# Prompt attention in 64 steps of two query tiles each, with q and k stored as halves by their projection

## The reference

```python
def stick_breaking(q, k, v, sb_bias, q_pos, k_pos):
    z = jnp.einsum('bqhd,bkhd->bhqk', q.astype(jnp.float32), k.astype(jnp.float32)) * (HEAD_DIM_SB ** -0.5)
    z = z + sb_bias.astype(jnp.float32)[None, :, None, None]
    mask = k_pos[None, :] < q_pos[:, None]
    log_1mb = jnp.where(mask, jax.nn.log_sigmoid(-z), 0.0)
    suffix = lax.cumsum(log_1mb, axis=3, reverse=True) - log_1mb
    a = jnp.where(mask, jnp.exp(jax.nn.log_sigmoid(z) + suffix), 0.0)
    o = jnp.einsum('bhqk,bkhd->bqhd', a, v.astype(jnp.float32))
    return o.astype(v.dtype)
```

## Time and profile before

| | us |
|---|---|
| runs, median (lowest to highest) | 3154.99 (3153.28 to 3155.18) |
| the profiled execution | 3153.76 |
| its span, first to last instruction | 3152.2 |
| attention stage, first sigmoid to the next stage's first transfer | 549.27 to 1198.18 |

### The profile page before, as it was taken

How to read it: one execution, slowest core, us unless ns; L and a number is a source line. 1 busy time by engine, 2 the same in 40 slices (tenths; PEclk the granted TensorE clock), 3 DMA queues, 4 the chain that set the end, 5 groups by cost and what they waited for, 6 DMA issues and landing times.

```text
span 3152.2 us, 51506 instructions
## 1 busy us (share of the span) xinstructions
PE 3035.5 (96%) x18364; PEld 2805.3 (89%) x18364; DVE 2062.2 (65%) x2820; ACT 1645.0 (52%) x2375; POOL 149.1 (5%) x277
## 2 busy tenths in 40 slices
PE   8999999888888889999999999999999999999998
PEld 6888887776677669999999999999999999999998
DVE  4222422888987897775677756777477774778845
ACT  5444311997888885543445534455344543444433
POOL 0000000112311220000000000000000000000000
PEclk9999999999999999999999999999999999999999
DMA  5224334554755555443364334543445434444432
GB/s 185 93 93 137 108 114 120 139 135 133 202 129 134 137 169 156 118 120 112 110 183 120 114 114 130 164 119 111 116 142 154 115 113 117 143 127 120 115 112 78
DMA packets 584224, 405.90 MB, mean 129 GB/s; under 512 B 38489, under 2 KB 547842, under 8 KB 584034
## 3 DMA queue, kind: packets, MB, share of 16 engines
q1 hardware_dynamic: 543012, 301.45, 33.8%
q0 software_dynamic: 20544, 67.19, 7.4%
q10 hardware_dynamic: 20512, 35.17, 3.2%
HBM read 358.87 MB, written 44.87 MB: 128 GB/s over the span
## 4 chain that ended last, share of the span: by engine, by line
PE 62%; DVE 0%; issue 0%; DVEq 0%; ACT 0%; ACTq 0%
PE pf_acc L60 20%; PE pf_acc L58 20%; PE pf_acc L59 20%; PE pf_ps_t L1720 1%; PE pf_ps_sum L1659 0%; PE pf_ps_sum L1668 0%; PE pf_ps_sum L1673 0%; PE pf_ps_t L1730 0%; PE pf_ps_t L1791 0%; DVE late_c L2066 0%; DVE late_ssum L1998 0%; DVEq L1596 0%; DVE late_u L1988 0%; DVE pf_h L2192 0%; ACT late_sq L1819 0%
## 5 line engine op out<-in xcount | busy, mean ns | idle before, releaser
L1812 ACT ACTIVATE late_w_hi<-ahead_raw 128x1024 fp32r<-128x1024 f32 x439 | 463.8, 1057 | 536.7 <-PE pf_acc L60 533.9
L60 PE MATMUL pf_acc<-pf_x_hi,late_w_lo 128*128 128x416 f32 x2080 | 734.1, 353 | 0.0
L58 PE MATMUL pf_acc<-pf_x_hi,late_w_hi 128*128 128x416 f32 x2080 | 733.1, 352 | 0.0
L59 PE MATMUL pf_acc<-pf_x_lo,late_w_hi 128*128 128x416 f32 x2080 | 726.0, 349 | 0.0
L1982 DVE TENSOR_TENSOR late_w_lo<-ahead_raw,late_w_hi 128x1024 fp32r<-128x1024 f32 x439 | 536.1, 1221 | 269.8 <-ACT late_w_hi L1812 269.0
L58 PE MATMUL pf_acc<-late_f_hi,late_w_hi 128*128 128x416 f32 x1280 | 453.4, 354 | 3.2 <-DVEq L2205 3.2
L60 PE MATMUL pf_acc<-late_f_hi,late_w_lo 128*128 128x416 f32 x1280 | 451.9, 353 | 0.0
L59 PE MATMUL pf_acc<-late_f_lo,late_w_hi 128*128 128x416 f32 x1280 | 447.6, 350 | 0.0
L59 PEld LDWEIGHTS pf_acc<-pf_x_lo,late_w_hi 128*128 128x128 f32 x2080 | 390.8, 188 | 7.9 <-issue 1.6
L58 PEld LDWEIGHTS pf_acc<-pf_x_hi,late_w_hi 128*128 128x128 f32 x2080 | 390.5, 188 | 3.7 <-issue 1.6
L60 PEld LDWEIGHTS pf_acc<-pf_x_hi,late_w_lo 128*128 128x128 f32 x2080 | 390.0, 187 | 2.3
(11 more groups left out here) (248 smaller groups left out, 3971.9 us busy)
## 6 DMA issues: line engine op xcount, KB each, us to landing
ahead_raw<-in_w_up_dram SPq DMA_DIRECT2D x220, 512.0 KB, 4.0
ahead_raw<-in_w_down_dram SPq DMA_DIRECT2D x80, 512.0 KB, 4.0
high_pages<-in_cache_k_dram POOLq DMA_DIRECT2D x128, 256.0 KB, 3.5
ahead_raw<-in_w_out_dram SPq DMA_DIRECT2D x40, 512.0 KB, 5.3
ahead_raw<-in_w_ple_gate_dram SPq DMA_DIRECT2D x40, 512.0 KB, 4.0
high_pages<-in_cache_v_dram POOLq DMA_DIRECT2D x64, 256.0 KB, 3.4
at_kT<-in_cache_v_dram POOLq DMA_DIRECT2D x64, 256.0 KB, 4.1
ahead_raw<-in_w_down_dram SPq DMA_DIRECT2D x40, 384.0 KB, 3.5
```

The lines of the kernel that those rows point to most:

```text
L58: nc.tensor.matmul(out, stat_hi, mov_hi, start=first, stop=False)
L59: nc.tensor.matmul(out, stat_hi, mov_lo, start=False, stop=False)
L60: return nc.tensor.matmul(out, stat_lo, mov_hi, start=False, stop=last)
L1812: nc.scalar.activation(w_hi[k % 4][:, :], raw[k % 4][:, :], ACT.Copy).then_inc(hi_split, 1)
```

## The change

Query tiles m and 15-m make one step: together they have 17 key tiles for every m, so there are 64 steps of 2176 columns. The columns stand in the order long tile, short tile, and a step has three granules of 768, 768 and 640 columns (`EDGES`). VectorE runs two running products in a step, one for each tile, and one weighting. A step has five groups of transposes (4, 4, 4, 4 and 1 tiles), and these now alternate with the granules. `project_qk` splits q and k after its transposes and stores both halves (QH, QL, KH, KL); `load_operands` fetches them with six transfers for each head (the first head's first 1536 columns already in `project_qk`), and `operands` and `keys_high` are gone. `units_of` spreads the units evenly over the steps 3 to 61. Some small buffers and the work that prepares the next stage are moved. The core of the diff:

```diff
+def load_operands(eng, D, tiles, h, cols, loaded):
+    q2, k_hi, k_lo = (f32(t[:, cols]) for t in tiles)
+    rows = slice(64 * h, 64 * h + 64)
+    for part in range(2):
+        half = slice(64 * part, 64 * part + 64)
+        eng.dma_start(q2[half, :], D[("QH", "QL")[part]][rows, cols]).then_inc(loaded, 16)
+        eng.dma_start(k_hi[half, :], D["KH"][rows, cols]).then_inc(loaded, 16)
+        eng.dma_start(k_lo[half, :], D["KL"][rows, cols]).then_inc(loaded, 16)
...
-                sp.dma_start(dst[:, :, bass.ds(at, P)], src[s][:, :, :]).then_inc(stored[s], 16)
+                sp.dma_start(to_hi[:, :, bass.ds(at, P)], hi[s][:, :, :]).then_inc(stored[s], 16)
+                sp.dma_start(to_lo[:, :, bass.ds(at, P)], lo[s][:, :, :]).then_inc(stored[s], 16)
...
+                    dve.wait_ge(stored[s], 32 * stores)
+                banked = src[:, :].rearrange("p (k t) -> p k t", k=4)
+                nc.vector.tensor_copy(hi[s][:, :, :].bitcast(F32R), banked).then_inc(high, 1)
+                dve.wait_ge(high, n)
+                nc.vector.tensor_tensor(lo[s][:, :, :].bitcast(F32R), banked, hi[s][:, :, :], ALU.subtract).then_inc(ready, 1)
...
-            q2, q_raw, half = front["q2"], front["q_raw"], slice(0, 1024)
-            dve.wait_ge(raw_loaded, 64)
-            nc.vector.tensor_copy(q2[:, half], q_raw[:, :]).then_inc(q_high, 1)
...
-            dve.wait_ge(q_high, 1)
-            nc.vector.tensor_tensor(q2[64:P, half], q_raw[64:P, :], f32(q2[64:P, half]), ALU.subtract)
-            dve.wait_ge(k_high, 1)
-            nc.vector.tensor_tensor(front["k_lo"][:, half], front["k_raw"][:, :], f32(front["k_hi"][:, half]), ALU.subtract)
...
     HEADS, NQ, LAG = 8, 16, 3
-    STEPS = HEADS * NQ
+    PER = NQ // 2
+    STEPS = HEADS * PER
+    TILES, GRANULES, RUNS = NQ + 1, 3, 5
+    WIDTH = P * TILES
+    EDGES = (0, 768, 1536, WIDTH)
...
+    def short_tile(s):
+        return s % PER if s // PER == HEADS - 1 else PER - 1 - s % PER
+    def long_tile(s):
+        return NQ - 1 - short_tile(s)
...
-    total_keys = sum(keys_of(s) + 300 for s in range(3, STEPS - 2))
     units_of = [[] for _ in range(STEPS + LAG + 2)]
-    t, run, placed = 3, keys_of(3) + 300, 0
+    t, placed, first_unit, last_unit = 3, 0, 3, STEPS - 3
     for g in range(GROUPS):
         for u in range(UNITS):
             if apart(u) and units_of[t]:
-                for _ in range(2 if u in (U_TURN, U_MIX) else 1):
-                    t += 1
-                    run += keys_of(t) + 300
-            while t < STEPS - 3 and run * GROUPS * UNITS < placed * total_keys:
+                t += 2 if u in (U_TURN, U_MIX) else 1
+            while t < last_unit and (t + 1 - first_unit) * GROUPS * UNITS < placed * (last_unit - first_unit):
                 t += 1
-                run += keys_of(t) + 300
             units_of[t].append((g, u))
             placed += 1
...
-    def first_turns(t):
+    def turns(t):
         s = t - LAG
-        return min(groups[s], max(1, 3 - len(turned_fills(t)))) if has(s) else 0
+        if not has(s):
+            return [range(0)] * (GRANULES + 1)
+        first = max(1, 3 - len(turned_fills(t)))
+        ends = [first, first + 1, first + 2, RUNS]
+        return [range(a, b) for a, b in zip([0] + ends, ends)]
     order = []
...
+                def load(h):
+                    if h >= 2:
+                        sp.wait_ge(z_ready, granule(PER * (h - 1), 0))
+                    load_operands(sp, D, [t[h % 2] for t in (q2, k_hi, k_lo)], h, slice(0, 2048), qk_loaded[h % 2])
...
                 def logits(s, g):
-                    i, h = s % NQ, s // NQ
...
+                    border = P * (long_tile(s) + 1)
+                    for c in range(EDGES[g], EDGES[g + 1], BANK):
+                        end = min(c + BANK, EDGES[g + 1])
+                        parts = [(c, min(end, border), long_tile(s), c)] if c < border else []
+                        if border < end:
+                            parts.append((max(c, border), end, short_tile(s), max(c, border) - border))
+                        parts.sort(key=lambda part: part[1] - part[0])
+                        for a, b, tile, k0 in parts:
+                            w, z0 = max(b - a, 2 * P), a - EDGES[g]
+                            turned = b - a == P and b - c == BANK
+                            last = scores(z, z0 - P if turned else z0, w, q2[h % 2][:, tile * P:(tile + 1) * P], h, k0, turned, b in (border, WIDTH))
+                            if b in (border, WIDTH):
+                                last = nc.tensor.matmul(z[:, b - P - EDGES[g]:b - EDGES[g]], ident_b[:, :], far_b[:, :], start=False, stop=True)
                     last.then_inc(z_ready, 1)
...
+                            tiles = long_tile(s + e) + 1
+                            kt, end, at = (n, tiles - 1, P) if n < tiles else (n - tiles, NQ - tiles, 0)
+                            last = nc.tensor.matmul(ps_o[64 * e:64 * e + 64, at:at + P], v[h % 2][:, kt, :], aT[(s + e) % 3][:, n, :],
+                                                    start=kt == 0, stop=kt == end, tile_position=(0, 64 * e))
...
-                        for r in range(first_turns(t)):
+                    for g in range(GRANULES + 1):
+                        for r in turns(t)[g]:
                             turn(s, r)
-                    if has(t):
-                        for g in range(granules[t]):
+                        if has(t) and g < GRANULES:
                             logits(t, g)
-                    if has(s):
-                        for r in range(first_turns(t), groups[s]):
-                            turn(s, r)
+                    if has(s - 2) and s % 2 == 0:
...
                 def sigmoid(t, g):
-                    n = keys_of(t)
-                    at = granule(t, g)
-                    w = min(n - 1024 * g, 1024)
+                    at, h = granule(t, g), t // PER
+                    c0, w = EDGES[g], EDGES[g + 1] - EDGES[g]
                     act.wait_ge(z_ready, at + 1)
-                    nc.scalar.activation(beta[t % 3][:, 1024 * g:1024 * g + w], ps_z[at % 2][:, 0:w], ACT.Sigmoid, bias=bias[t // NQ % 2][:, :])
-                    c0, skip = (0, 1) if g == 0 else (1023, 0)
+                    nc.scalar.activation(beta[t % 3][:, c0:c0 + w], ps_z[at % 2][:, 0:w], ACT.Sigmoid, bias=bias[:, h:h + 1])
+                    c0, skip = (0, 1) if g == 0 else (c0 - 1, 0)
                     nc.scalar.activation(rest[t % 4][:, c0:c0 + w - skip], ps_z[at % 2][:, skip:w], ACT.Sigmoid, scale=-1.0,
-                                         bias=minus_bias[t // NQ % 2][:, :]).then_inc(b_done, 1)
...
-                    if has(s):
-                        for r in range(first_turns(t)):
+                    for g in range(GRANULES + 1):
+                        for r in turns(t)[g]:
                             take(s, r)
-                    if quad_end(s - 2):
-                        quad_out((s - 2) // 4)
-                    if has(t):
-                        sigmoid(t, 0)
-                    if has(s):
-                        for r in range(first_turns(t), groups[s]):
-                            take(s, r)
-                    if has(t) and granules[t] == 2:
-                        sigmoid(t, 1)
-                    if t % NQ == PART_AT[0] and t // NQ + 1 < HEADS:
-                        keys_high(2 * (t // NQ + 1))
-                    if t % NQ == PART_AT[1] and t < STEPS:
-                        keys_high(2 * (t // NQ) + 1)
-                    if t == STEPS:
+                        if g == 0 and pair_end(s - 2):
+                            pair_out((s - 2) // 2)
...
-                        act.wait_ge(a_done, STEPS)
                         act.wait_ge(join["raw_loaded"][0], 16)
...
-                    if t == STEPS + 2:
+                    if t == STEPS + LAG + 1:
...
-                def operands(n, part):
-                    slot = n // 2 % 2
-                    src = slice(0, HALF)
-                    cols = slice(n % 2 * HALF, n % 2 * HALF + HALF)
-                    if part == 0:
-                        dve.wait_ge(loaded, 64 * n + 64)
-                        nc.vector.tensor_copy(q2[slot][:, cols], q_raw[:, src]).then_inc(q_high, 1)
-                    if part == 1:
-                        dve.wait_ge(q_high, n + 1)
-                        nc.vector.tensor_tensor(q2[slot][64:P, cols], q_raw[64:P, src], f32(q2[slot][64:P, cols]), ALU.subtract)
-                        if n % 2 == 0 and n:
-                            biases_of(n // 2)
-                    if part == 2:
-                        dve.wait_ge(k_high, n + 1)
-                        nc.vector.tensor_tensor(k_lo[slot][:, cols], k_raw[:, src], f32(k_hi[slot][:, cols]), ALU.subtract).then_inc(half_ready, 1)
...
+                    end = P * (long_tile(s) + 1)
+                    dve.wait_ge(b_done, granule(s, [end <= edge for edge in EDGES].index(True) - 1) + 3)
```

(4 more changed lines are left out.)

242 lines of the change are left out of this document (101 added, 141 removed).

## The result

The changed kernel takes 3203.12 us (median of 4 runs, 3195.55 to 3206.12) against 3155.09 of the kernel before on the same chip: the ratio is 1.0149, with an interval of 1.0130 to 1.0167. It is 48 us slower. The forecast of 3160, and with it the whole range up to 3185, was too low.

What follows compares the result with a forecast made beforehand. No engine is full; TensorE and ScalarE take turns as the bound. Stage +1.1, start +1.4 and tail -2.6 make 0; 5 us for the clock gives 3158.8, and the median's 1.2 gives 3160, range 3112 to 3185 (own 3148 to 3172).

Steps and rivals of the forecast that it cites:

- the walk: Attention stage stepped through by instruction prices: 15.4 us for two equal steps without units, 628.2 us for the stage.
- VectorE's dropped work: Attention stage: 15 casts and 30 subtractions fewer on VectorE, costed at nothing; busy time lower by some 45 us.
- The two places: Steps 26 and 55: eight sums in a row wait for pages of values, some 16 us lost in each.
- the clock: TensorE's clock falling in the attention stage, mostly idle at the page waits; 5 us added to the forecast.
- Then pairs with two sums at 18.3: Step pairs behind the eight sums in a row, with two sums in each step: 18.3 us per pair.
- the sentence on the next head's load: SyncE's load of the next head, 3 MB instead of 2 MB, stands ahead of this head's stores and lands in time.
- the start: End of `project_qk`: last subtraction and a second transfer delay the end of that stage by some 1.4 us.
- the tail: From the last sigmoid to the next stage: 19.2 us against 21.8 before, so -2.6.
- rival 2: Sums in steps 26 and 55: pages are not waited for, or other engines' lists fill the time; 3130, chance 0.15.
- rival 3: Attention stage: ten more clock falls of 3.4 us, +17, giving 3176; decides below mean clock 0.94; chance 0.25.
- Its other place: Odd steps where TensorE waits for the third granule: clock falls there, each costing up to 1.7 us.
- a sign of being wrong: The prediction counts as wrong if `project_qk` ends more than 3 us later.

Runs made afterwards that it cites:

- the early load: Changed kernel with only the transfers of the next head's q and k moved two stores earlier in SyncE's list: 3191.9 us (1.0117).
- the last one: Changed kernel with all head loads spread over six steps, units placed and half of the `ahead_mix` transfer earlier: 3131.9 us (0.9926).

## Why the prediction was wrong

**What bounds the kernel, and the walk.** Right in kind, and a little short everywhere. Steps 20 and 21 took 16.05 us (15.4 forecast), steps 4 and 5 took 20.2 (19.9), and ScalarE idled for 2.1 behind the weighing (1.3 forecast). The first row is step 20's first sigmoid, the second step 22's:

```profile
746.37 0.93 ACT L1313 ACTIVATE at_beta<-at_ps_z,keep_sb_bias 128x768 f32<-128x768 f32 x1
...
762.42 0.93 ACT L1313 ACTIVATE at_beta<-at_ps_z,keep_sb_bias 128x768 f32<-128x768 f32 x1
```

**VectorE's dropped work costs nothing.** Right; shown by 57 us that cost 0.6. Its busy time in the stage is 491.6 us, 66 less than before and not 45.

**The two places.** The mechanism was right: 16 us each were forecast, and put into the kernel before it costs 15.1 each. Between the equal steps it costs more. With the early load the kernel takes 3191.9, and with the sums two to a step and the load in pieces 3147.9: 44 us for both places, with the clock behind them, where the prediction had 32 and 5.

**"Then pairs with two sums at 18.3".** This is the step that failed. Steps 28 to 31 took 53.2 us where two such pairs would have been 36.6. Behind it stands the sentence on the next head's load, that it "is through long before the first store is due, and has a whole head's time to land". It was costed at nothing. In SyncE's list the load of head 4 stands behind the last stores of head 2, which come from the weighing at the end of step 27, so SyncE issued it at 842.5, in the middle of head 3, and its 3 MB lay in the queues together with the values' pages. I had asked whether the load comes in time, never what it delays. Moved away it gives 11 us back, and spread over six steps 10 more where two sums stand in a step. The page "DMA: Bandwidth & Descriptors" of the Trainium skill (Issuing engines are not separate DMA queues) says that transfers started by SyncE and by GpSimd run on the same engines and interleave. The trace agrees: the awaited pages took 14.6 and 18.9 us to land against 3.3.

**The sum over both.** The forecast of 3160 was 3123 without the waits, 32 for the waits and 5 for the clock. The kernel at 3147.9, where no sum waits for a page and no load is in the way, stands for the first term, which was 25 too low. The other two were 37 and are 55 (3203.1 - 3147.9), 18 too low: 11 for the load, 7 for the two places and the clock. So the missing 43 us are not one mistake. Of the 25, about 15 are the walk (610.8 us from the first sigmoid to the last in that kernel, against 628.2 less 32), 3 the start and 6 the tail, both below. The prediction's rival 2 (pages not waited for, 3130) is that kernel's case, and it missed by 18. A part of the 15 belongs to the experiment and not to the change: with two sums to a step the second group's keys are packed eight pages to a step in steps 36 to 38.

**The clock.** 5 us were added for it. It stood at half for 20.5 us in steps 26 and 55 alike and for 17.1 us in steps 29 and 30, and the stage's mean was 0.94, where rival 3 begins to decide. Rival 3's place "behind the page waits" was right. Its other place gave little. In steps 3 to 19 TensorE idles for up to 2.4 us in a step, in pieces of about 1 us, and the clock fell twice, for 3.4 us each. One fall, with the stretch ahead of it:

```profile
569.80:576.90 7.10, 4.68 (x35) 3.76 (x34) 7.07 (x4) 6.95 (x12) 1.27 (x3) 1.00 1.00 211
576.90:580.30 3.40, 3.40 (x16) 3.21 (x15) 3.37 (x3) 2.21 (x5) 1.19 (x3) 0.50 0.93 336
```

The other 169.8 of these 176.6 us ran at the higher level, steps with the same idle among them. The rule of the Trainium skill that is cited at rival 3 says that such small idles can let the clock swing; the trace agrees for two steps of seventeen, at a price of at most 1.7 us each by the prediction's own figure, which is little of the 43. In the kernel of 3147.9 the stage has 0.98, and in the last one 0.99. How much of the 55 us is the clock's alone no run separates.

**Edges.** The start was put at +1.4 and is +4.1, more than the 3 us that the prediction named as a sign of being wrong. The last store is issued 1.9 us later (545.57 for 543.64) and takes 4.2 us to land in place of 2.3, so that the first transfer of `attend` comes 5.8 us behind it, before 4.0. The tail was put at 19.2 and is 25.3; the walk had products and weighings in it, but not the transfer of `ahead_mix`, which now waits for a late store.

## What to carry to other kernels

Where small jobs are hung onto steps by a share of the way done, look at the largest number in one step, and compare it with the pace of what feeds it: here one sum for 4.6 us of page issues. A burst cost its own wait here, and the clock fell behind it. When a transfer grows or moves, ask first which other transfers are in the queues then; issuing it early gave 11 us, and issuing it in pieces, one in each step, 10 more. Fewer sums in a step gave most: 34 us from eight to two, with the early load in both. And an engine without idle time isn't yet on the path: put work onto it and see.
